# Unit keys of the recurrent layer, channel tile by channel tile, with scaling, squares and roots on ScalarE

## The reference, cut to what matters

```python
def rwkv_inputs(u, shift_w, w0, w2, a0, a2, g2, k_k, k_a):
    ...
    logw = (w0 + jnp.einsum('btdr,drc->btdc', jnp.tanh(lw), w2)).astype(jnp.float32)
    ...
    kk = (k * k_k).reshape(B, T, RW_HEADS, RW_N).astype(jnp.float32)
    kk = kk * lax.rsqrt(jnp.sum(kk * kk, -1, keepdims=True) + 1e-12)
    ...
    g = jax.nn.sigmoid(lg) @ g2
```

## Time and profile before

| | us |
|---|---|
| median of 3 runs | 4211.17 (4208.52 to 4217.72) |
| profiled execution | 4217.04 |
| its span, first to last instruction | 4215.2 |
| the stage `head_unit_keys` in it | 1556.9 to 1595.4 |

### The profile page before, as it was taken

The page is one execution under the profiler, slowest core; times in us unless marked ns, Lnnn a source line. Parts: engine busy times, 40 slices in busy tenths (PEclk is TensorE's granted clock), DMA queues, the critical chain, the costliest instruction groups (busy, mean ns, idle before and its releaser), DMA issues. The chain is left out here.

```text
span 4215.2 us, 70162 instructions
## 1 busy us (share of the span) xinstructions
PE 3678.9 (87%) x29588; PEld 2620.8 (62%) x29588; DVE 2002.5 (48%) x3720; ACT 1101.5 (26%) x2219; POOL 640.1 (15%) x675
## 2 busy tenths in 40 slices
PE   5978869999979897989868777698999997899999
PEld 4844663444458774868753222297778776677877
DVE  3688750000045566757660000155567446656762
ACT  2124510000024313223220000124532223663221
POOL 0014400111113202415200000013200001440000
PEclk8988989999989998989979999999999998899999
DMA  4142258999940321010249999820122231012222
GB/s 169 61 158 61 76 212 329 393 391 391 377 148 36 98 100 53 3 42 3 69 181 394 402 405 403 336 81 21 47 95 95 93 98 42 21 35 73 94 95 80
DMA packets 195487, 659.98 MB, mean 157 GB/s; under 512 B 27708, under 2 KB 86076, under 8 KB 145368
## 3 DMA queue, kind: packets, MB, share of 16 engines
q1 hardware_dynamic: 182392, 621.16, 38.8%
q0 software_dynamic: 12784, 34.35, 3.1%
HBM read 626.01 MB, written 29.44 MB: 155 GB/s over the span
## 5 line engine op out<-in xcount | busy, mean ns | idle before, releaser
L3469 DVE TENSOR_TENSOR ffn_w_lo<-ffn_landing,ffn_w_hi 128x1024 fp32r<-128x1024 f32 x128 | 156.8, 1225 | 295.4 <-ACT ffn_w_hi L3447 295.4
L3418 PE MATMUL ffn_ps<-ffn_inT_hi,ffn_w_hi 128*128 128x512 f32 x704 | 277.8, 395 | 3.5 <-PEq L70 3.5
L3418 PE MATMUL ffn_ps<-ffn_inT_lo,ffn_w_hi 128*128 128x512 f32 x704 | 278.8, 396 | 0.0
L3418 PE MATMUL ffn_ps<-ffn_inT_hi,ffn_w_lo 128*128 128x512 f32 x704 | 277.9, 395 | 0.0
L2044 PE MATMUL up_ps<-w_quarter,rowsT 128*64 128x512 f32 x1024 | 235.9, 602 | 36.7 <-DMA w_quarter<-in_moe_w 36.7
L2044 PE MATMUL down_ps<-w_quarter,hiddenT 128*64 128x512 f32 x1024 | 235.0, 598 | 31.7 <-DMA w_quarter<-in_moe_w 29.7
L2044 PE MATMUL gate_ps<-w_quarter,rowsT 128*64 128x512 f32 x1024 | 235.5, 605 | 29.5 <-DMA w_quarter<-in_moe_w 20.7
L1960 POOL DMA_INDIRECT summed_dram<-gains_then_rows,part_row x48 | 74.7, 1556 | 929.2 <-DVE gains_then_rows L2174 924.3
L2167 DVE TENSOR_TENSOR gain_then_hidden<-up_ps,gain_then_hidden 128x768 f32<-128x768 f32 (+1 forms) x32 | 26.4, 824 | 348.3 <-PE up_ps L2056 179.0
L2044 PEld LDWEIGHTS down_ps<-w_quarter,hiddenT 128*64 128x64 f32 x1024 | 68.5, 136 | 189.3 <-issue 130.1
L2104 ACT ACTIVATE rowsT<-misc_ps 128x384 f32<-128x384 f32 (+1 forms) x64 | 27.8, 437 | 599.0 <-PE misc_ps L2033 597.3
(11 more groups left out here) (722 smaller groups left out, 8416.8 us busy)
## 6 DMA issues: line engine op xcount, KB each, us to landing
w_quarter<-in_moe_w SPq DMA_DIRECT2D x384, 1024.0 KB, 17.8
ffn_landing<-in_f_w_up SPq DMA_DIRECT2D x88, 512.0 KB, 3.5
ada_ring<-in_ada_w SPq DMA_DIRECT2D x80, 512.0 KB, 5.6
ffn_landing<-in_f_w_down SPq DMA_DIRECT2D x44, 512.0 KB, 3.5
w_landing<-in_od_w_in SPq DMA_DIRECT2D x13, 1024.0 KB, 6.3
w_landing<-in_a_w_in SPq DMA_DIRECT2D x12, 1024.0 KB, 5.1
ada_landing<-in_ada_w SPq DMA_DIRECT2D x8, 1024.0 KB, 12.6
w_landing<-in_ev_w_in SPq DMA_DIRECT2D x6, 1024.0 KB, 5.0
```

Of the source, the lines that this page charges most:

```text
L3418: mm = nc.tensor.matmul(ps[c % 4][:, :], w[:, c % NP, cols], h[:, k, :], start=(k + i == 0), stop=(k == KD - 1 and i == 2))
L3469: nc.vector.tensor_tensor(wl[:, c % NP, :], land[:, c % NL, :], wh[:, c % NP, :].bitcast(F32), ALU.subtract).then_inc(split, 1)
```

## The change

Keys, squares and roots move to ScalarE, one channel tile at a time, and the roots read the sums from PSUM with the constant 1e-12 as a bias from a column `eps` that VectorE sets. VectorE inverts and multiplies tile by tile. On TensorE the eight sums now stand ahead of the first chunk of the modulation rows and wait, tile by tile, for the squares; from the fifth on a sum waits for the root that empties its bank. On ScalarE tanh and sigmoid now come after the roots and the first `keep_partial`.

```diff
--- before.py
+++ after.py
@@ -2928,16 +2928,19 @@
     with Stage(nc) as st:
         sq = st.sb("squares", [P, 4, TOK])
         inv = st.sb("inverse_norm", [P, 4, TOK])
+        eps = st.sb("eps", [P, 1])
         ps = [st.ps(f"norm_ps{i}", [P, 512]) for i in range(4)]
-        ready = st.sem("squares_ready")
+        eps_ready = st.sem("eps_ready")
+        squared = st.sem("squared")
         summed = st.sem("summed")
-        kept = st.sem("kept")
         root = st.sem("root_ready")
+        keyed = st.sem("keys_ready")
         chained = st.sem("chained")
         landed = st.sem("landed")
         chunks = range(4)
         mod_ps = [st.ps(f"ada_ps{i}", [P, 512]) for i in range(4)]
         block = st.block()
+        units = [(j, r) for j in range(4) for r in ((0, SEQ), (SEQ, TOK))]
 
         @block.sync
         def _(sp):
@@ -2947,31 +2950,34 @@
             mod.store(sp, chunks)
             sp.wait_ge(mod.stored, 80)
             sp.wait_ge(landed, 16 * len(loads))
-        units = [(j, r) for j in range(4) for r in ((0, SEQ), (SEQ, TOK))]
-
-        @block.vector
-        def _(dve):
-            chain = Chain(dve, chained)
-            wide = [P, 4, TOK]
-            chain(nc.vector.tensor_tensor(kk[:, :, :], U[:, 4:8, :], cst["k_k"].unsqueeze(2).broadcast_to(wide),
-                                          ALU.mult))
-            nc.vector.tensor_tensor(sq[:, :, :], kk[:, :, :], kk[:, :, :], ALU.mult).then_inc(ready, 1)
+
+        @block.scalar
+        def _(act):
+            for j in range(4):
+                nc.scalar.activation(kk[:, j, :], U[:, 4 + j, :], ACT.Copy, scale=cst["k_k"][:, j:j + 1]).then_inc(keyed, 1)
+                act.wait_ge(keyed, j + 1)
+                nc.scalar.activation(sq[:, j, :], kk[:, j, :], ACT.Square).then_inc(squared, 1)
+            act.wait_ge(eps_ready, 1)
             for u, (j, (a, b)) in enumerate(units):
-                dve.wait_ge(summed, u + 1)
-                nc.vector.tensor_scalar(inv[:, j, a:b], ps[u % 4][:, 0:b - a], 1e-12, None, ALU.add).then_inc(kept, 1)
-            dve.wait_ge(root, 1)
-            chain(nc.vector.reciprocal(inv[:, :, :], inv[:, :, :]))
-            chain(nc.vector.tensor_tensor(kk[:, :, :], kk[:, :, :], inv[:, :, :], ALU.mult))
+                act.wait_ge(summed, u + 1)
+                nc.scalar.activation(inv[:, j, a:b], ps[u % 4][:, 0:b - a], ACT.Sqrt, bias=eps[:, :]).then_inc(root, 1)
+            mod.keep_partial(act, 0, mod_ps)
+            nc.scalar.activation(T[:, 0, :], T[:, 0, :], ACT.Tanh)
+            nc.scalar.activation(T[:, 2, :], T[:, 2, :], ACT.Sigmoid)
+            for c in chunks[1:]:
+                mod.keep_total(act, c - 1, mod_ps)
+                mod.keep_partial(act, c, mod_ps)
+            mod.keep_total(act, 3, mod_ps)
 
         @block.tensor
         def _(pe):
-            mod.partial(pe, 0, mod_ps)
-            pe.wait_ge(ready, 1)
             for u, (j, (a, b)) in enumerate(units):
                 if u >= 4:
-                    pe.wait_ge(kept, u - 3)
+                    pe.wait_ge(root, u - 3)
+                pe.wait_ge(squared, j + 1)
                 nc.tensor.matmul(ps[u % 4][:, 0:b - a], cst["pair_ones"], sq[:, j, a:b], start=True, stop=True) \
                     .then_inc(summed, 1)
+            mod.partial(pe, 0, mod_ps)
             mod.partial(pe, 1, mod_ps)
             for c in chunks[2:]:
                 mod.total(pe, c - 2, mod_ps)
@@ -2979,17 +2985,14 @@
             for c in chunks[2:]:
                 mod.total(pe, c, mod_ps)
 
-        @block.scalar
-        def _(act):
-            nc.scalar.activation(T[:, 0, :], T[:, 0, :], ACT.Tanh)
-            nc.scalar.activation(T[:, 2, :], T[:, 2, :], ACT.Sigmoid)
-            mod.keep_partial(act, 0, mod_ps)
-            act.wait_ge(kept, len(units))
-            nc.scalar.activation(inv[:, :, :], inv[:, :, :], ACT.Sqrt).then_inc(root, 1)
-            for c in chunks[1:]:
-                mod.keep_total(act, c - 1, mod_ps)
-                mod.keep_partial(act, c, mod_ps)
-            mod.keep_total(act, 3, mod_ps)
+        @block.vector
+        def _(dve):
+            chain = Chain(dve, chained)
+            nc.vector.memset(eps[:, :], 1e-12).then_inc(eps_ready, 1)
+            for j in range(4):
+                dve.wait_ge(root, 2 * j + 2)
+                chain(nc.vector.reciprocal(inv[:, j, :], inv[:, j, :]))
+                chain(nc.vector.tensor_tensor(kk[:, j, :], kk[:, j, :], inv[:, j, :], ALU.mult))
 
 
 GN_EPS = 64e-5
```

## The result

The changed kernel took 4232.88 us (median of six runs, 4223.34 to 4236.9); the kernel before 4216.59 (six runs, 4208.52 to 4223.9; three of them are those that the prediction knew). The medians are 16.3 us apart. The ratio, which is not the quotient of the medians, is 1.0036, with a 95% interval from 1.0019 to 1.0053: slower by 15.2 us, and by 8 to 22. The prediction said 4217.3, 6.1 us slower, in a range that ended at 4224. So the sign was right, and size and time were not.

What follows compares the result with a forecast made beforehand. The stage was taken as bound by VectorE until 1595.36, with the modulation chain close behind at 1594.2. Terms 1571.1 + 8.1 + 7.25 + 6.3 + 8.7 = 1601.45, 6.1 us longer; 4211.2 + 6.1 = 4217.3 us, range 4208 to 4224.

Steps and rivals of the forecast that it cites:

- The stage's sum: Unit keys stage: start of the second chunk's loads plus later waits end it at 1601.45 instead of 1595.36, 6.1 us longer.
- the first load: SyncE's first issue for the second chunk of modulation weights, after the sums of squares: 1571.1, bounds 1569.5 and 1573.2.
- the rounds: Modulation weights: time from one chunk's last piece to the next's; two rounds, 7.25 and 6.3 us.
- VectorE, ScalarE, the table: Unit keys stage: VectorE ends near 1590, ScalarE's last square at 1563.8, table load of 1.28 until 1565.1.
- the table rule's rival: ScalarE's table switch costs some 2.66 us with a drain; stage 7.5 us longer, 4218.7 us; chance 0.05.
- Fast clock, and the next stage gains: TensorE enters the next stage at 2.4 GHz, 3.9 us come back; kernel 2.2 us faster, about 4209; chance 0.08.
- Slow clock throughout: TensorE gets 1.2 GHz for sums, partial sums and totals; both rounds 7.25; 9 to 11 us, about 4221.5; chance 0.20.
- The moved order costs nothing: Modulation chain still ends by 1594.2, so the stage gains VectorE's 1.1 us: 4210.1; chance 0.05.

Runs made afterwards that it cites:

- order_alone: Kernel before with only the new order: eight sums ahead of the first chunk on TensorE, that chunk's copy behind the root on ScalarE; 4224.24 us, ratio 1.0015.
- idle6: Kernel before with one more reciprocal of 128x928 behind VectorE's last product in the unit keys stage; 4226.76 us, ratio 1.0016.
- idle54: Kernel before with an added reciprocal of 128x832 at the end of VectorE's chain in the unit keys stage; 4225.86 us, ratio 1.0015.
- after_pad09: Changed kernel with a second memset of 128x1024 in the short stage behind the unit keys; 4222.99 us, ratio 1.0010 against the kernel before.
- after_pad18: Changed kernel with a second memset of 128x2048 in the short stage behind the unit keys; 4226.52 us, ratio 1.0013 against the kernel before.
- chunks_between: Changed kernel with the first chunk ahead of the sums and the second between the fourth and fifth sum on TensorE; 4219.24 us, ratio 1.0002.
- chunk0_first: Changed kernel with one call moved: the first chunk's partial sum ahead of the eight sums again on TensorE; 4215.11 us, ratio 0.9994.
- chunks_spread: Changed kernel with the calls for the chunks spread between those for the tiles on TensorE and ScalarE; 4217.52 us, ratio 0.9996.

## Why the prediction was wrong, point by point

| kernel | stage, us | first scan, us | total against before, us |
|---|---|---|---|
| before, twice | 0 | 216.00, 213.17 | 0, -3.8 |
| changed, three times | +5.97, +6.03, +5.84 | 217.89, 217.79, 217.87 | +15.2, +9.7, +7.2 |
| order_alone | +6.48 | 213.17 | +6.3 |
| idle6 | +5.99 | 213.24 | +6.7 |
| idle54 | +5.39 | 217.80 | +6.3 |
| after_pad09 (stage and memset) | +5.23 + 1.18 | 213.13 | +4.2 |
| after_pad18 (stage and memset) | +6.79 + 2.25 | 213.29 | +5.5 |
| chunks_between | -1.64 | 213.22 | +0.8 |
| chunk0_first | -1.86 | 216.05 | -2.5 |
| chunks_spread | -3.18 | 212.94 | -1.7 |

(Totals are the ratio less 1, times 4216; each is uncertain by 4 to 7 us.)

*The stage's sum*, 6.1, was right: 5.97, and each of its terms. The sums end at 1570.1 (1570.0), the first load at 1571.16 (1571.1), its last piece 7.9 later (8.1), the rounds 7.20 and 6.48 (7.25 and 6.3), and from the last piece to the landed store 8.4 (8.7). chunk0_first and order_alone show the cause from both sides.

*VectorE, ScalarE, the table*: right, to 0.4 us; the table rule's rival fell on the load that starts 0.02 behind the square. *Fast clock, and the next stage gains*: its first twelve matmuls took 8.02 again, so nothing came back. *Slow clock throughout*: its condition was half true. The second half of the sums took 4.54 of the 5.1 that half clock would take, but the rounds did not lengthen. *The moved order costs nothing*: refuted by the first load.

*The step that failed* is the end of the sum: "with 6.1 more it is 4223.1", that is, that what a stage loses is what the kernel loses, with later stages at nothing. Only a rival gave a later stage a price (the next one's first twelve matmuls), and the sum put the rest at nothing without a reason. The first scan is 217.8 to 217.9 us in all three profiles of the changed kernel, and 216.00 and 213.17 in two of the kernel before. With it the change would cost 6.0 + 1.9 = 7.9 to 6.0 + 4.7 = 10.7 us, which fits the 9.7 and 7.2 of the two longer comparisons and lies at the low end of the interval of the first one (8 to 22). Singly their intervals have 6.0 too, together they lie just above it (9.0, with 6.5 to 11.5): a loss beyond the stage is likely, and the timed runs don't show that it is the scan's. That the place of the slow stretch decides the scan's length is shown in profiles: idle54 and idle6 differ by 0.6 us of added work and by 4.6 us of scan. That it decides the timed total is not shown, since their medians are level.

*The base* was the second mistake. "I put the change onto the median" meant 4211.17, a median of three runs; the kernel before was 4216.59 in six, and 4216.11, 4219.53 and 4220.23 in some thirty each. So of the miss of 15.6 us, 5.4 came from the base (4216.59 - 4211.17), which the profiled execution, 4217.04, had contradicted, and 10.2 from the change (16.3 - 6.1). Of these the scan has 1.9 to 4.7. The remaining 5 to 8 were not there in the later comparisons, and a median of six runs that span 14 us can lie that far off; a cause in the kernel was not found. A part goes with the clock: the three slowest of the six (4234.05 to 4236.9) have granted clocks of 0.934 and 0.935 on record, the other three, with 0.938 and 0.939, a mean of 4227.6, which is 11.2 above that of before (4216.4). So low a clock stands in 3 of the 24 later runs of the changed kernel and in 3 of the 99 of the kernel before that were timed beside them; that three of the six had it is put down to chance here, which is not shown. The second scan of the first profile, 4.9 us longer, was 0.9 longer in the next and not longer in the third.

What stays open is why the clock falls at the end of the scan in some alignments and not in others, in what share of the executions, and so how much of the loss beyond the stage's 6 us is the scan's.

## What to carry to other kernels

When an engine's order changes, look for the buffers that this engine frees: here eight sums of squares ahead of the first chunk's matmuls kept the ring full and its first load back by 11.9 us (that load is 14.53 us behind ScalarE's first row, and was 2.68 behind it), and that outweighed a VectorE chain that became 5.3 us shorter (33.20 instead of 38.47 from the same row). Do not add a small change to the median of three runs: put it on the mean of all that is known, the profiled execution included, and make the range as wide as the runs. The stage's own loss was forecast to 0.1 us from rows (6.1, measured 5.97), and that closeness was in part luck: the same code lost 5.23 to 6.79 us in the five profiles that have it. In after_pad09 the last two rows of totals took 1.02 and 1.60 us at a granted clock of 0.74, in after_pad18 1.87 and 1.86 us at 0.50. The whole kernel can be forecast here only to some 5 us.

## What the runs showed of the hardware

A stage that no edit touches was 213 or 216 to 218 us long, and the granted clock went with it (0.94, and 0.92 or 0.91). In the long ones its last 12 to 14 us ran at 0.58 to 0.63, in idle6 and after_pad09 at 1.00. The Trainium skill's page "TensorE: Matmul & The Clock Gate", Part 1, has the array at 1.2 GHz until activity releases it. That fits the sums after a long wait (0.64 in order_alone); it doesn't say which of two nearly equal schedules gets the slow end of a scan, and a decay stage that began some 0.45 us later, counted from the start of the unit keys stage (after_pad09 against the changed kernel), was enough to move from one to the other.
